# A conditioned retention and RG-LRU step: seven block products in place of eight for pairs of tiles of the first MLP matrix

## What is computed

```python
for l in range(DEPTH):                                   # 2 layers
    ada = jax.nn.silu(c) @ w_ada[l] + b_ada[l]           # shifts, scales and gates
    h = rmsnorm(x, norm1_g[l]) * (1.0 + sc1) + sh1
    mix, ... = mixer(h, ...)                             # retention and RG-LRU, w_in, w_proj_*, w_out
    x = x + gt1 * mix
    h2 = rmsnorm(x, norm2_g[l]) * (1.0 + sc2) + sh2
    x = x + gt2 * (jnp.square(jax.nn.relu(h2 @ w_mlp1[l])) @ w_mlp2[l])
y = rmsnorm(x, final_g)
```

## Time and profile before

| what | value |
|---|---|
| median of three timed runs | 2067.03 us (2064.87 to 2067.42) |
| span of the profiled execution | 2065.2 us |
| TensorE matmuls busy | 2040.9 us (99%), 14848 instructions |
| TensorE weight loads busy | 1925.7 us (93%) |
| VectorE busy | 1064.9 us (52%) |
| ScalarE busy | 728.1 us (35%) |
| GpSimd busy | 243.7 us (12%) |
| mean data rate | 113 GB/s |

### The profile page before, as it was taken

One profiled execution on the slowest core, in us unless ns is written; L12 is line 12 of the kernel. 1 busy time (PEld: TensorE's weight loads), 2 busy tenths in 40 slices (PEclk: granted clock), 3 DMA queues, 4 the chain that ended last, 5 costly groups with the idle time before them and its releaser, 6 DMA issues.

```text
span 2065.2 us, 35331 instructions
## 1 busy us (share of the span) xinstructions
PE 2040.9 (99%) x14848; PEld 1925.7 (93%) x14848; DVE 1064.9 (52%) x1676; ACT 728.1 (35%) x915; POOL 243.7 (12%) x265
## 2 busy tenths in 40 slices
PE   6999999999999999999999999999999999999998
PEld 3869989999998999999988798999999899999998
DVE  5525566774446444444464355667735453535353
ACT  3124444665223222222231354456632321212122
POOL 0001120000032011000320011100000320101014
PEclk9999999999999999999999999999999999999999
DMA  8523342222262232323522314422222622222223
GB/s 354 184 71 108 97 158 91 80 82 82 82 244 103 82 123 82 123 82 123 218 89 69 106 66 138 133 81 85 81 82 82 240 74 90 82 82 83 82 82 108
DMA packets 78920, 232.61 MB, mean 113 GB/s; under 512 B 7360, under 2 KB 27840, under 8 KB 78528
## 3 DMA queue, kind: packets, MB, share of 16 engines
q1 hardware_dynamic: 57168, 205.71, 28.4%
q10 hardware_dynamic: 21616, 24.93, 3.7%
HBM read 218.52 MB, written 12.09 MB: 112 GB/s over the span
## 4 chain that ended last, share of the span: by engine, by line
PE 96%; DVE 2%; DMA 1%; issue 0%; SPq 0%; ACT 0%; POOL 0%; DVEq 0%; POOLq 0%
PE acc L1321 81%; PE acc L1487 4%; PE misc L1416 2%; PE misc L1606 2%; DVE tmp L859 1%; PE misc L1567 1%; PE acc L1386 1%; PE misc L1496 1%; DMA first_raw<-ada_in 1%; DVE h_lo L846 1%; PE misc L1540 1%; PE misc L1543 1%; PE acc L1394 1%; PE misc L1542 1%; PE misc L1560 0%; PE misc L1527 0%
## 5 line engine op out<-in xcount | busy, mean ns | idle before, releaser
L1321 PE MATMUL acc<-h_hi,weight_h 128*128 128x288 f32 x2688 | 793.9, 297 | 0.0
L1321 PE MATMUL acc<-h_hi,weight_l 128*128 128x288 f32 x2688 | 786.7, 295 | 0.0
L1321 PE MATMUL acc<-h_lo,weight_h 128*128 128x288 f32 x2688 | 786.3, 294 | 0.0
L424 ACT ACTIVATE weight_h<-raw 128x1024 fp32r<-128x1024 f32 x286 | 303.1, 1060 | 1069.4 <-PE acc L1321 967.2
L812 DVE TENSOR_TENSOR weight_l<-raw,weight_h 128x1024 fp32r<-128x1024 f32 x286 | 398.0, 1391 | 259.0 <-ACT weight_h L424 258.5
L1321 PEld LDWEIGHTS acc<-h_hi,weight_h 128*128 128x128 f32 x2688 | 502.7, 188 | 9.4 <-issue 6.5
L1321 PEld LDWEIGHTS acc<-h_lo,weight_h 128*128 128x128 f32 x2688 | 502.6, 188 | 0.8
L1321 PEld LDWEIGHTS acc<-h_hi,weight_l 128*128 128x128 f32 x2688 | 502.4, 188 | 0.0
L1321 PE MATMUL acc<-b_hi,weight_l 128*128 128x288 f32 x1520 | 419.0, 294 | 0.0
L1321 PE MATMUL acc<-b_hi,weight_h 128*128 128x288 f32 x1520 | 418.3, 294 | 0.0
L1321 PE MATMUL acc<-b_lo,weight_h 128*128 128x288 f32 x1264 | 345.9, 294 | 0.0
(11 more groups left out here) (232 smaller groups left out, 1900.8 us busy)
## 6 DMA issues: line engine op xcount, KB each, us to landing
raw<-stream SPq DMA_DIRECT2D x290, 512.0 KB, 3.4
ada_raw<-ada_in SPq DMA_DIRECT2D x48, 512.0 KB, 6.2
first_raw<-ada_in SPq DMA_DIRECT2D x36, 512.0 KB, 14.5
s_s<-state_in ACTq DMA_DIRECT2D x8, 1024.0 KB, 6.6
ret_s_out<-s_s ACTq DMA_DIRECT2D x8, 1024.0 KB, 4.4
two_raw<-ada_in SPq DMA_DIRECT2D x12, 512.0 KB, 10.5
x<-x_in ACTq DMA_DIRECT2D x1, 2304.0 KB, 13.3
wrg<-wrg_in ACTq DMA_DIRECT2D x16, 128.0 KB, 2.8
```

The costliest lines, as they stand in the source:

```text
L424: A(weight_h[:, j % 2, :], raw[:, (j + 2) % 4, :], ACT.Copy).then_inc(h_split, 1)
L1321: last = M(acc[j % 2][:, half, 0:HALF], w, r[:, k, half * HALF:(half + 1) * HALF], start=(k == 0 and n == 0), stop=(k == KT - 1 and n == 2))
```

## The change

In quarters 1 to 3 of both layers, the first half takes its eight tiles as four pairs. With the 1024 input features cut in two, the two tiles in two and the tokens in two, a pair is a product of 2 by 2 blocks, each block product 4 row blocks by 3 products, 12 matmuls of 288 columns. Eight such products are 96 matmuls; the change makes seven, 84 matmuls, by sums of blocks (Winograd's form of Strassen's product). Their names are q1, q2, q3, p4, r5, r6 and q7.

- **Token side**, once per layer: VectorE forms three sums of quarters of `h` and replaces one quarter of `h` by a fourth (`sum_quarters`, ten instructions on 128x1152), ScalarE rounds four (`round_quarters`), in the second half of quarter 0.
- **Weight side**, per pair: VectorE forms four sums of 128x512 blocks in three instructions (`sums_31` on 128x1024, `sum_2`, `sum_4`), in two new buffers of `raw`. A unit of two products has one 128x1024 slot of four in `weight_h` and `weight_l` (`high_unit` on ScalarE, `low_unit` on VectorE), so a pair has 3.5 units where it had 2 tiles.
- **Result side**, per pair: q1 goes to `misc`; ScalarE copies q1, q7 and one partial sum (`copy_q1`, `copy_q7`, `copy_u2`, 128x288 each), takes the ReLU of two blocks from PSUM (`cut_11`, `cut_12`) and of the other two in `tmp` (`cut_z`); VectorE adds the other two blocks (`add_z`); GpSimd squares twice 128x576, as before; ScalarE rounds (`round_u`) and VectorE subtracts (`low_u`), as before.
- The group of `w_ada` products of quarters 1 to 3 moves into the second half. The tables of `const` move into the two new buffers of `raw` and are loaded again for layer 1. The second half's fifth tile now takes the halves of the tokens one after the other.

```diff
+FAST_ORDER = (("q1", 0), ("q7", 0), ("r6", 0), ("q2", 0), ("p4", 0), ("r5", 0),
+              ("q1", 1), ("q7", 1), ("q3", 0), ("r6", 1), ("q2", 1), ("p4", 1), ("r5", 1),
+              ("q1", 2), ("q7", 2), ("q3", 1), ("r6", 2), ("q2", 2), ("p4", 2), ("r5", 2),
+              ("q1", 3), ("q7", 3), ("q3", 2), ("r6", 3), ("q2", 3), ("r5", 3), ("p4", 3), ("q3", 3))
...
-        raw = place("raw", [128, 4, 1024])
-        weight_h = place("weight_h", [128, 2, 1024], F32R)
-        weight_l = place("weight_l", [128, 2, 1024], F32R)
+        raw = place("raw", [128, 6, 1024])
+        weight_h = place("weight_h", [128, 4, 1024], F32R)
+        weight_l = place("weight_l", [128, 4, 1024], F32R)
...
+                def high_unit(qt, u):
+                    if u >= 4:
+                        act.wait_ge(product_done, n * PRODUCTS + 2 * u - 6)
...
+                            act.wait_ge(sums_ready, (n * 4 + p) * 3 + {"q7": 1, "r5": 1, "r6": 2, "q3": 3}[name])
+                    A(unit_part(weight_h, u), unit_source(u), ACT.Copy).then_inc(unit_high, 1)
...
+                    def copy_q1(p):
+                        done("q1", p)
...
+                        A(acc[p % 2][:, 1, 0:HALF], misc[:, p % 2, 0:HALF], ACT.Copy).then_inc(q1_copied, 1)
...
+                    def cut_z(p):
+                        act.wait_ge(z_done, n * 4 + p + 1)
+                        A(fast_tile(p, 1), fast_tile(p, 1), ACT.Relu, scale=-1.0).then_inc(z_cut, 1)
...
+                def low_unit(qt, u):
+                    dve.wait_ge(unit_high, fast_round(lay, qt) * UNITS + u + 1)
+                    V.tensor_tensor(unit_part(weight_l, u), unit_source(u), unit_part(weight_h, u).bitcast(F32), ALU.subtract).then_inc(unit_low, 1)
...
+                    def add_z(p):
+                        done_with("r5", p)
+                        dve.wait_ge(u2_copied, n * 4 + p + 1)
+                        dve.wait_ge(q7_copied, n * 4 + p + 1)
+                        V.tensor_tensor(fast_tile(p, 1), acc[p % 2][:, :, 0:HALF], kept_sums[:, p % 2], ALU.add).then_inc(z_done, 1)
...
+                    add_z(0)
+                    low_unit(qt, 6)
+                    sums_31(qt, 2)
+                    low_unit(qt, 7)
+                    sum_2(qt, 2)
+                    sum_4(qt, 2)
+                    low_u(0, 1)
+                    low_unit(qt, 8)
+                    low_u(0, 0)
+                    low_unit(qt, 9)
+                    sums_31(qt, 3)
+                    add_z(1)
...
+                    for p in range(4 if qt else 0):
+                        pool.wait_ge(z_cut, pairs + 1)
+                        G.tensor_tensor(fast_tile(p, 1), fast_tile(p, 1), fast_tile(p, 1), ALU.mult).then_inc(u_squared, 1)
+                        pool.wait_ge(c11_read, pairs + 1)
+                        pool.wait_ge(c12_read, pairs + 1)
+                        G.tensor_tensor(fast_tile(p, 0), fast_tile(p, 0), fast_tile(p, 0), ALU.mult).then_inc(u_squared, 1)
...
+                        for k in range(4):
+                            for c, (w, r) in enumerate(((wh, rhs_hi), (wh, rhs_lo), (wl, rhs_hi))):
+                                last = M(out, w, r[:, k, :], start=(first and k == 0 and c == 0), stop=(k == 3 and c == 2), skip_group_check=True)
+                        last.then_inc(product_done, 1)
...
+                        product("q1", p, quarter(h_hi, 0, 0), quarter(h_lo, 0, 0), misc[:, p % 2, 0:HALF], True)
...
+                        product("q7", p, t3_hi, t3_lo, acc[p % 2][:, 0, 0:HALF], True)
+                        if p:
+                            pe.wait_ge(z_done, pairs)
+                            q3(p - 1)
+                        pe.wait_ge(q1_copied, pairs + 1)
+                        product("r6", p, t2_hi, t2_lo, acc[p % 2][:, 1, 0:HALF], False)
+                        product("q2", p, quarter(h_hi, 1, 0), quarter(h_lo, 1, 0), misc[:, p % 2, 0:HALF], False)
+                        if p < 3:
+                            p4(p)
+                            r5(p)
```

More of the change, by code:

```diff
@@ L168, in build @@
         p_ms = place("p_ms", [128, 128])
[L169 removed]
+        const = place("const", [128, NFIRST])
         small = place("small", [128, DEPTH, NSMALL])
@@ L193, in cst @@
             a, b = _off[name]
+            if a >= NFIRST:
+                return tables[0:rows, a - NFIRST:b - NFIRST]
             return const[0:rows, a:b]
@@ L311, in halves, with quarter, fast_tile, unit_source @@
             return row.rearrange("p (a b) -> p a b", a=2)
+        def quarter(tile, kh, th):
+            return tile[:, 4 * kh:4 * kh + 4, half_cols(th)]
+        def fast_tile(p, n):
+            return tmp[:, 2 * (p % 2) + n, :].rearrange("p (a b) -> p a b", a=2)
+        def unit_source(u):
+            first, second = unit_blocks(u)
+            return blocks[:, first:second + 1:second - first, :]
+        def unit_part(tile, u):
+            return tile[:, unit_slot(u), :].rearrange("p (a b) -> p a b", a=2)
         def lru_rows(m):
@@ L329, in load_range @@
                         sp.wait_ge(l_split, lay * LAYER_TILES + i * 4 + (first + j + 1))
-                        load(lay * LAYER_TILES + i * 4 + (first + j + 4), j)
+                        load(lay * RAW_TILES + i * 4 + (first + j + 4), j)
             def load_ada(n, before):
@@ L702, in _ @@
                 for qt in range(QUARTERS):
[L703 to L707, removed]
+                    if qt == 0:
+                        for m in range(8):
+                            split_h(lay, AT_MLP, 0, m)
+                            ada_in_mlp(qt, m)
+                            act.wait_ge(u_ready, lay * 8 + m + 1)
+                            A(one(b_hi, m), tmp[:, 2 + m % 2, :].rearrange("p (a b) -> p a b", a=2), ACT.Copy).then_inc(u_rounded, 1)
+                    else:
+                        fast_high(qt)
                     if qt == QUARTERS - 1 and lay == 0:
@@ L1137, in _, with low_second @@
                 norm(2 * lay + 1, scale2, 3 * KT)
-                for qt in range(QUARTERS):
[L1139 to L1146, removed]
+                def low_second(qt, m):
+                    n = lay * LAYER_TILES + second_tile(qt) + m
+                    r = AT_MLP + qt * 16 + 8 + m
+                    dve.wait_ge(h_split, n + 1)
+                    V.tensor_tensor(weight_l[:, m % 2, :], raw[:, r % 4, :], weight_h[:, m % 2, :].bitcast(F32), ALU.subtract).then_inc(l_split, 1)
@@ new lines, in sums_31 @@
+                def sums_31(qt, p):
+                    base = 4 * (p % 2)
+                    reread(qt, p, "r5")
+                    for r in range(2):
+                        tile = lay * RAW_TILES + AT_MLP + qt * 16 + 2 * p + r
+                        dve.wait_ge(raw_loaded[tile % 4], 16 * (tile // 4 + 1))
+                    V.tensor_tensor(blocks[:, SUM_3:SUM_1 + 1, :], blocks[:, base:base + 4:3, :], blocks[:, base + 2:base + 3, :].to_broadcast([128, 2, 512]), ALU.add).then_inc(sums_ready, 1)
@@ new lines, in _ @@
+                for qt in range(QUARTERS):
+                    if qt == 0:
+                        with dve.Fori(0, 2) as i:
+                            for j in range(4):
+                                n, m = lay * 32 + i * 4 + j, i * 4 + j
+                                done(lay, AT_MLP, i, j)
+                                V.tensor_scalar(tmp[:, j % 2, :].rearrange("p (a b) -> p a b", a=2), acc[j % 2][:, :, 0:HALF], 0.0, None, ALU.max).then_inc(acc_free, 1)
+                                split_l(lay, AT_MLP, i, j)
+                                dve.wait_ge(u_rounded, n + 1)
+                                V.tensor_tensor(one(b_lo, m), tmp[:, 2 + j % 2, :].rearrange("p (a b) -> p a b", a=2), one(b_hi, m).bitcast(F32), ALU.subtract).then_inc(u_split, 1)
+                    else:
+                        fast_low(qt)
@@ L1309, in _, with stream_tile @@
                 pe.sem_inc(one_more, 1)
-            def stream_tile(lay, off, i, j, rhs_hi, rhs_lo, ready=None):
+            def stream_tile(lay, off, i, j, rhs_hi, rhs_lo, ready=None, order=range(KT)):
                 pe.wait_ge(l_split, lay * LAYER_TILES + i * 4 + (off + j + 1))
@@ L1320, in k_step @@
                         for half in halves:
-                            last = M(acc[j % 2][:, half, 0:HALF], w, r[:, k, half * HALF:(half + 1) * HALF], start=(k == 0 and n == 0), stop=(k == KT - 1 and n == 2))
+                            last = M(acc[j % 2][:, half, 0:HALF], w, r[:, k, half * HALF:(half + 1) * HALF], start=(k == order[0] and n == 0), stop=(k == order[-1] and n == 2))
                     return last
                 if ready is not None:
-                    for k in range(KT):
-                        ready(k)
+                    for n, k in enumerate(order):
+                        ready(n)
                         last = k_step(k, (0, 1))
@@ L1329, in stream_tile @@
                     for half in range(2):
-                        for k in range(KT):
```

(1 more changed line is left out.)

360 lines of the change are left out of this document (317 added, 43 removed).

## The result

The changed kernel takes 2050.80 us (median of 4 runs, 2050.19 to 2051.65) beside 2066.01 us for the kernel before: 0.9928 of it, 95% interval 0.9914 to 0.9942, 15.2 us less. The forecast was 33.3 us less, 2033.7 us (from the 2067.03 of the first three runs), with a range up to 2045.

A forecast was written before the change was run, and what follows sets the result against it. TensorE, busy 99% of the span, was taken as the bound before and after. Matmuls saved, -38.1 us, plus six stops, +4.8, gave -33.3 us: from 2067.03 to 2033.7 us, range 2028 to 2045.

The forecast's parts named there:

- The saving: In 24 pairs, TensorE loses 12 matmuls each, 288 at 0.1324 us, 38.1 us, all on the path.
- The forecast stop: Before q3 of pair 1, TensorE waits for `add_z(1)`: 0.8 us per fast part, 4.8 us in six.
- the walk: VectorE's and ScalarE's queues timed from r5(0), 9.73 us, to the end of `add_z(1)`, 24.3 us, against q3 at 23.83.
- the other pairs are on time: Elsewhere in the fast part, `add_z` of pairs 0, 2 and 3 was said to finish before TensorE needs it.
- the copies before r6, p4 and r5: ScalarE's copies in the fast part were said to be ready with 0.5 us or more to spare.
- the third: GpSimd kept out: VectorE's next instruction precedes the waiting square, 3.3 us per fast part, 2048.7 us; chance 0.12.
- the second rival: Each square in the fast part blocks VectorE for its whole length, 1.15 us, not 0.75; 2038.5 us; chance 0.15.
- The slower case: Units and `sums_31` at half speed on split blocks make VectorE the bound, 57.8 us per fast part; 2109 us; chance 0.05.
- VectorE's load: VectorE's summed work in a fast part, 41.3 us of 44.49, leaving TensorE the bound.
- The sign: To show the forecast right, VectorE was to be busy over 80% of a fast part.

The follow-up runs named there:

- the kernel without stops: Changed kernel with VectorE's unit 2 low part and pair 1 sums a tile earlier, and `add_z` of pair 1 before pair 3's sums; 2029.36 us.
- add first: Changed kernel with VectorE taking `add_z` of pair 1 before the sums for pair 3; 2048.27 us.
- no squares: Changed kernel with GpSimd's squares in the fast parts cut to one column, so quarters 1 to 3 are not squared; 2048.35 us.
- copies first in layer 1 only: Changed kernel with ScalarE copying q1 and q7 of pair 0 before rounding unit 3, in layer 1 alone; 2047.52 us.
- copies first: Changed kernel with ScalarE copying q1 and q7 of pair 0 before rounding unit 3, in both layers; 2038.92 us.
- both orders: Changed kernel with ScalarE's q1 and q7 copies before unit 3 and VectorE's `add_z` of pair 1 before pair 3's sums; 2032.22 us.
- sums a tile earlier: Changed kernel with VectorE's low part of unit 2 and sums for pair 1 moved one tile earlier; 2034.63 us.

## Why the prediction was wrong

**The saving was right.** 288 x 0.1324 = 38.1 us; the kernel without stops is 36.7 us below the kernel before. The products start 0.13 us apart also where they carry waits: 44.6 us for 28 of them against 44.49.

**The forecast stop was right.** The two `add_z` in the changed kernel's timeline of VectorE:

```profile
1754.30 0.76 DVE L1433 TENSOR_TENSOR tmp<-acc,kept_sums 128x576 f32<-128x576 f32 x1 [0.58 <-PE acc L2029]
...
1768.24 0.75 DVE L1433 TENSOR_TENSOR tmp<-acc,kept_sums 128x576 f32<-128x576 f32 x1
```

From the news of r5(0), 1754.30, to the end of `add_z(1)`, 1769.0, it took 14.7 us; the walk had 24.34 - 9.73 = 14.6. That they agree so closely is in part luck: the two squares cost 1.78 us where the walk had 1.50, and the overlaps of instructions that follow each other, which it left at nothing, took most of that back. The stop was priced at 0.8 us and measured 0.72. It was put down to VectorE's order and the squares: either one undone removes it.

**The step that failed** is the sentence that "the other pairs are on time", with "the copies before r6, p4 and r5 0.5 us or more" to spare. The prediction shows its walk only from r5(0) on; how it came to 0.5 us at the start of the part is not written out, and it is possible only if ScalarE's rounding of unit 3 waits for nothing but its buffer, 0.2 us into the part. The order rows ahead of the prediction show that a unit also waits for VectorE where it holds sums, and unit 3 holds one. By the prediction's own prices it would have been: news of the last tile 0.2, `gated_add` 1.09, unit 2 1.23, `sums_31(1)` 1.23, rounding of unit 3 1.06, copy of q1 0.50 at most (0.39 as measured): 5.2 to 5.3 us, where r6(0) is due after two products, at 3.18. That is 2.0 to 2.1 us late, measured 2.09. Making that sum 5.2 us earlier (it starts 2.9 us before the last `gated_add` instead of 2.3 us after it) removed it. This is the larger part of the miss, 13.2 of 18.1 us in six fast parts, and the term that the sum had at nothing.

**What was missing altogether** is the clock. The forecast took 2.4 GHz throughout, as the rows of before show it in the MLP, but there TensorE never stood for 2 us. The clock's dips, 4.5 us, are the other part.

**The rivals.** The time lies next to the third (2048.7 us) by chance, for its mechanism did not happen. GpSimd was not kept out: between VectorE instructions that follow each other closely, the square got its turn at the first boundary. The changed kernel's rows of the first square, and the sum that the second one stretched:

```profile
1755.39 1.23 DVE L1377 TENSOR_TENSOR weight_l<-raw,weight_h 128x1024 fp32r<-128x1024 f32 x1 [0.34 <-ACT weight_h L802]
1756.65 2.05 DVE L1392 TENSOR_TENSOR raw<-raw 128x1024 f32<-128x1024 f32 x1
...
1761.02 1.63 DVE L1398 TENSOR_TENSOR raw<-raw 128x512 f32<-128x512 f32 x1
...
1756.01 1.61 POOL L1669 TENSOR_TENSOR tmp<-tmp 128x576 f32<-128x576 f32 x1 [62.23 <-ACT tmp L847]
```

The square waits for L1377 to end at 1756.6, needs 1.0 us more, to 1757.62, and the sum behind it, 1.22 us when alone, ends 1.08 us later. In all six fast parts it is the same: each of the 30 squares that came while VectorE was in an instruction waited for that one alone and then needed 1.0 us. A square cost VectorE 0.83 and 0.95 us in the chain, between the 0.75 taken and the 1.15 of the second rival. The rule of the Trainium skill that the second rival rested on ("SBUF — State Buffer", section "Who interferes with whom": the one that issues first holds the other off for its whole duration) fits these rows, too. The second rival's price was too high, since a square that has waited needs only 1.0 us more. The slower case did not happen either: the block sums of two strided pieces take 1.22 us, as one plain piece does.

**VectorE's load** was priced too high. The sign was that it is busy over 80% of a fast part, 41.3 us; the window of the changed kernel's part says 35.0 us of 47.5, 74%, and in the kernel without stops it was 32.5 of 44.6:

```profile
1742.36:1789.88 47.52, 45.15 (x339) 44.68 (x338) 35.02 (x37) 25.62 (x42) 9.46 (x7) 1.00 0.35 112
```

The 41.3 gave each of eight squares a delay of 0.75 us, 6.0 in all, where three delays of 0.83, 0.95 and 0.95 us, 2.7 in all, are in the part; and it counted eight `low_u`, of which six lie in it. These two make 4.8 of the 6.3 us.

## What to carry to other kernels

When an in-order queue gets new work with waits, walk it from its first instruction after the seam with the stage before, not from the middle: at the seam it also has to finish what the stage before leaves (here one `gated_add`, one unit and one sum). A short copy that TensorE needs within two products must not stand behind a long instruction that waits for a third engine; either give it the earlier place or, better, make the third engine's piece ahead of the seam. And a stop of TensorE of about 2 us may cost more than itself (here 1.5 us on top in 14 of 21 cases), so remove those first.

## What the runs showed of the hardware

After stops of 2.2 us the clock fell to 1.2 GHz in 14 of 21 cases (changed kernel 3 of 6, add first 4 of 6, no squares 4 of 6, copies first in layer 1 only 3 of 3) and cost 14 or so matmuls at 0.24 us, 1.5 us. The stops were alike, and in one trace of each kernel the dips lay in layer 0 alone, in both layers, or after all three stops that were left; what decides which stop is followed by one was not tried. After the 24 stops of 0.46 to 1.34 us in the three kernels that have no longer one (copies first 12, both orders 6, sums a tile earlier 6) no dip followed.
